# A two-block network on one core: gated-recurrence levels raised in two pairs of buffers and multiplied two by two; top-k masks formed by ScalarE

## The reference

```python
def dsa_mixer(...):                       # selected attention, 4 heads of 64
    s = einsum(q_idx, k_idx); score = sum_h w * relu(s)      # 8 index heads of 32
    score = where(causal, score, -1e30)
    _, sel = top_k(score, 128)            # only these keys are attended to
    logits = q.k * 64**-0.5, -1e30 where not valid; softmax; times v

def hgrn2_mixer(...):                     # recurrent heads, 4 of 128, chunks of 64
    G = cumsum(log_f) within a chunk
    A[i,j] = sum_d q[i,d] exp(G[i,d]-G[j,d]) k[j,d]   for j <= i
    o = A v + (q exp(G)) S ;  S = exp(G_last) S + (k exp(G_last-G))^T v
    rmsnorm(o) * silu(g)
```

## Time and profile before

| | |
|---|---|
| time, median of 3 runs | 1200.15 us (1198.34 to 1200.52) |
| the profiled execution | 1199.26 us, span 1197.5 us |
| busy share of the span | PE 99%, PEld 81%, DVE 67%, ACT 57%, POOL 38% |
| index scores and top-k to the start of the recurrent products | about 575 to 680 us |
| recurrent windows 0, 1, 2, 3 | about 680 to 705, to 739, to 777, to 805 us |
| mean granted TensorE clock | 0.998 |

### The profile page before, as it was taken

One profiled execution on the slowest core, in us unless ns is written; L12 is line 12 of the kernel. 1 busy time (PEld: TensorE's weight loads), 2 busy tenths in 40 slices (PEclk: granted clock), 3 DMA queues, 4 the chain that ended last, 5 costly groups with the idle time before them and its releaser, 6 DMA issues.

```text
span 1197.5 us, 19754 instructions
## 1 busy us (share of the span) xinstructions
PE 1183.4 (99%) x7102; PEld 964.1 (81%) x7102; DVE 807.4 (67%) x1839; ACT 687.8 (57%) x1333; POOL 459.0 (38%) x300
## 2 busy tenths in 40 slices
PE   9999999999999999999999999999999999999998
PEld 8777777777877777789777677778988889899897
DVE  6866767776777776766689866776761265475575
ACT  6766666675546778734567787653532353443542
POOL 0201111112520000053477697315354577576663
PEclk9999999999999999999999999999999999999999
DMA  5423354541543322352322112323363323223322
GB/s 202 159 71 106 91 174 141 159 159 53 194 121 113 95 96 92 121 160 71 114 71 71 37 54 71 123 89 120 128 193 106 106 71 118 94 100 112 106 72 71
DMA packets 41040, 131.82 MB, mean 110 GB/s; under 512 B 4576, under 2 KB 7264, under 8 KB 40944
## 3 DMA queue, kind: packets, MB, share of 16 engines
q1 hardware_dynamic: 35360, 121.39, 31.6%
q10 hardware_dynamic: 5584, 9.18, 2.5%
HBM read 127.10 MB, written 2.13 MB: 108 GB/s over the span
## 4 chain that ended last, share of the span: by engine, by line
PE 84%; DVE 8%; issue 4%; DMA 2%; ACT 2%; POOL 1%; SPq 0%; ACTq 0%; DVEq 0%; POOLq 0%
PE G L1069 17%; PE G L1071 16%; PE G L1070 16%; DVE adaw L3144 2%; PE G L2118 2%; PE S L1196 2%; PE G L2119 2%; PE G L2120 2%; DVE best L3143 2%; PE O L1256 2%; PE T L1235 2%; PE S L1413 1%; PE O L1476 1%; PE T L1460 1%; PE S L2119 1%
## 5 line engine op out<-in xcount | busy, mean ns | idle before, releaser
L1069 PE MATMUL G<-hi,wH 128*128 128x512 f32 x1032 | 419.0, 406 | 0.5 <-DVE xT L1164 0.4
L1071 PE MATMUL G<-hi,wL 128*128 128x512 f32 x1032 | 403.3, 391 | 0.0
L1070 PE MATMUL G<-lo,wH 128*128 128x512 f32 x1032 | 403.0, 390 | 0.0
L633 POOL TENSOR_TENSOR wL<-w,wH 128x1024 fp32r<-128x1024 f32 x89 | 219.9, 2476 | 440.1 <-ACT wH L2273 440.0
L1069 PEld LDWEIGHTS G<-hi,wH 128*128 128x128 f32 x1032 | 194.0, 188 | 55.6 <-issue 17.5
L1071 PEld LDWEIGHTS G<-hi,wL 128*128 128x128 f32 x1032 | 193.9, 188 | 42.2
L1070 PEld LDWEIGHTS G<-lo,wH 128*128 128x128 f32 x1032 | 194.4, 188 | 38.3 <-issue 1.9
L2273 ACT ACTIVATE wH<-w 128x1024 fp32r<-128x1024 f32 x140 | 147.2, 1054 | 103.8 <-DMA w<-weights_dram 53.8
L413 POOL TENSOR_TENSOR kd<-kd,band 128x256 f32<-128x256 f32 x8 | 6.5, 808 | 195.4 <-DMA kd<-c_dram 195.4
L2832 DVE TENSOR_TENSOR wL<-w,wH 128x1024 fp32r<-128x1024 f32 x51 | 62.3, 1222 | 11.0 <-ACT wH L2273 10.2
L1186 DVE CUSTOM_DVE_ANT_0 adaw<-adaw,scr 128x1024 f32<-128x1024 f32 x36 | 62.2, 1727 | 0.0
(11 more groups left out here) (560 smaller groups left out, 2564.8 us busy)
## 6 DMA issues: line engine op xcount, KB each, us to landing
w<-weights_dram SPq DMA_DIRECT2D x150, 512.0 KB, 3.6
adaw<-ada_dram SPq DMA_DIRECT2D x48, 512.0 KB, 4.3
wp<-weights_dram SPq DMA_DIRECT2D x20, 512.0 KB, 4.4
kd<-c_dram ACTq DMA_DIRECT2D x16, 512.0 KB, 4.8
xT<-x_dram SPq DMA_DIRECT2D x4, 512.0 KB, 8.1
out_dram<-xT SPq DMA_DIRECT2D x8, 256.0 KB, 2.2
scr<-ca_dram SPq DMA_DIRECT2D x2, 512.0 KB, 6.3
kd<-cbias SPq DMA_DIRECT2D x8, 128.0 KB, 4.4
```

What stands on the lines that cost most here:

```text
L633: g.tensor_tensor(wL[:, u.slot], raw_home(u), wH[:, u.slot].bitcast(f32), ALU.subtract).then_inc(w_lo, 1)
L1069: mm(home[:, :], whi, H[:, k, :], start=(k == first), stop=False)
L1070: mm(home[:, :], whi, L[:, k, :], start=False, stop=False)
L1071: last = mm(home[:, :], wlo, H[:, k, :], start=False, stop=(k == final))
```

## The change

- `raised(t, n)` names one of two pairs of rows: the first pair for n = 1, 2, 3, 6, 7, the second for n = 4, 5, 8. The raises n = 3, 5, 7 read one pair and write the other, so they don't wait for the product of their level; the half that they don't touch is copied by ACT (`leave`, three for each head, 128x512).
- PE makes the products 3 and 4 back to back, 5 and 6 too, and `turn_ke` directly behind product 7. The pieces of units between them are joined.
- DVE's and ACT's orders in the windows are rewritten: among others `silu_z(t)` and `gates(t + 1)` come after the joins of levels 5 and 6, and `rooted_h` before raise 4.
- The masks of selected attention: DVE's TENSOR_SCALAR is removed, ACT computes -x - 3e38 in place (`masks_c`), and `logits_c` waits for it. `scores_c(0)` moves two k-tiles into unit 11; `exps_c(2)` and `exps_c(3)` move ahead of other ACT work; two convolution taps move behind the last softmax turn.

```diff
+        def raised(t, n):
+            row = 2 - 2 * (t % 2) + (4 if n in (4, 5, 8) else 0)
+            return kd[:, row, :], kd[:, row + 1, :]
...
         def logits_c(dve, k):
             t, r = C_TURNS[k]
+            dve.wait_ge(*mark("i_mask", 3 - r))
...
+        def masks_c(act, q):
+            act.wait_ge(*mark("i_best", q))
+            part = sel[:, A_AT[q]:A_AT[q] + (q + 1) * P]
+            s.activation(part, part, ACT.Identity, scale=-1.0, bias=lowest[:, 0:1]).then_inc(sem("i_mask"), 1)
...
             def product(t, p):
                 pe.wait_ge(sem("h_x"), 8 * t + max(p, 1) + since("h_x"))
+                if p in (4, 6):
+                    pe.wait_ge(*mark("h_moved", 3 * t + p // 2 - 1))
...
             def first_window():
-                gemm_h(1, 0, (5,))
+                gemm_h(1, 0, (5, 6, 7))
                 product(0, 3)
-                gemm_h(1, 0, (6, 7))
                 product(0, 4)
-                gemm_h(1, 1, (0, 1))
+                gemm_h(1, 1, (0, 1, 2, 3))
                 product(0, 5)
-                gemm_h(1, 1, (2, 3))
                 product(0, 6)
-                gemm_h(1, 1, (4, 5))
+                gemm_h(1, 1, (4, 5, 6))
                 product(0, 7)
-                gemm_h(1, 1, (6, 7))
+                turn_ke(0)
+                gemm_h(1, 1, (7,))
...
             def window(t):
                 opened(t)
                 fill(t, 3)
+                fill(t, 4, (0, 1))
                 product(t, 3)
+                product(t, 4)
                 if t == 2:
                     conv_sum()
-                fill(t, 4)
-                product(t, 4)
+                fill(t, 4, (2, 3))
                 fill(t, 5)
                 product(t, 5)
+                product(t, 6)
                 if t == 2:
                     conv_sqsum()
                 fill(t, 6)
-                product(t, 6)
                 fill(t, 7, (0, 1))
                 product(t, 7)
+                turn_ke(t)
                 fill(t, 7, (2, 3))
...
             gemm_i(10)
+            gemm_i(11, (0, 1))
             scores_c(pe, 0)
-            gemm_i(11)
+            gemm_i(11, (2, 3, 4, 5, 6, 7))
...
+            def leave(t, n):
+                m = 1 << (n - 1)
+                act.wait_ge(sem("h_x"), 8 * t + n + since("h_x"))
+                if n == 3 and t > 1:
+                    act.wait_ge(sem("h_o"), t - 1 + since("h_o"))
+                s.activation(left_behind(t, m, n + 1), left_behind(t, m, n), ACT.Copy).then_inc(sem("h_moved"), 1)
...
                 terms(CONV_C[5], CONV_C[6])
+                leave(0, 3)
                 take_hv(0)
                 gate_1(0)
+                leave(0, 5)
                 conv_terms(0, 0)
                 split_h(4)
+                leave(0, 7)
                 forget(1)
...
                 conv_terms(t, 4)
+                leave(t, 5)
                 raw_h(t, 3, zraw, sem("h_silu"), t + since("h_silu"))
                 gate_1(t)
...
             def raise_both(t, n):
                 m = 1 << (n - 1)
-                dve.wait_ge(sem("h_products"), 8 * t + (2 if n == 1 else n + 1) + since("h_products"))
+                if n in (1, 2, 4, 6):
+                    dve.wait_ge(sem("h_products"), 8 * t + (2 if n == 1 else n + 1) + since("h_products"))
+                if n in (4, 6):
+                    dve.wait_ge(*mark("h_moved", 3 * t + n // 2 - 1))
...
-                link(v.tensor_scalar(part, part, -HUGE, NEG, ALU.not_equal, ALU.mult))
...
-                level_of(t, 2)
...
+                raise_both(t, 2)
+                raise_both(t, 3)
+                joined(t, 2)
...
+                else:
+                    rooted_h(t - 1)
+                raise_both(t, 4)
+                joined(t, 3)
+                if t == 2:
+                    conv_centre()
+                raise_both(t, 5)
+                joined(t, 4)
...
+                normed_h(t - 1)
+                raise_both(t, 6)
+                raise_both(t, 7)
+                joined(t, 5)
+                joined(t, 6)
                 gated_h(t - 1)
                 if t < 3:
                     silu_z(t)
+                    gates(t + 1)
```

More of the change, by code:

```diff
@@ L226, in build @@
         epsc = sb("epsc", [P, 1])
+        lowest = sb("lowest", [P, 1])
         vecT = sb("vecT", [P, N_VEC])
@@ L1897, in turn_ke @@
                 pe.wait_ge(sem("h_x"), 8 * t + 8 + since("h_x"))
+                pe.wait_ge(*mark("h_moved", 3 * t + 3))
                 pe.wait_ge(sem("h_v"), t + 1 + since("h_v"))
                 for c in range(3):
-                    last = nc.tensor.transpose(T[0][:, c * P:(c + 1) * P], raised(t)[1][:, c * P:(c + 1) * P], ident[:, :])
+                    last = nc.tensor.transpose(T[0][:, c * P:(c + 1) * P], raised(t, 8)[1][:, c * P:(c + 1) * P], ident[:, :])
                 last.then_inc(sem("h_keT"), 1)
@@ L1930, in outputs @@
                 for c in range(1, NQ):
-                    mm(O[:, c * P:(c + 1) * P], state[:, c - 1, :], raised(t)[0][:, c * P:(c + 1) * P], start=False, stop=False)
+                    mm(O[:, c * P:(c + 1) * P], state[:, c - 1, :], raised(t, 8)[0][:, c * P:(c + 1) * P], start=False, stop=False)
                 pe.wait_ge(sem("h_early"), t + 1 + since("h_early"))
@@ L2037, in last_window @@
                 opened(3)
-                fill(3, 3, (0, 1))
+                fill(3, 3)
                 product(3, 3)
-                fill(3, 3, (2, 3))
                 product(3, 4)
                 output_m(0, (4, 5))
+                output_m(1, (4, 5))
                 product(3, 5)
-                output_m(1, (4, 5))
                 product(3, 6)
                 output_m(0, (0, 1))
+                output_m(1, (0, 1))
                 product(3, 7)
-                output_m(1, (0, 1))
                 turn_ke(3)
@@ L2518, in _ @@
             raw(8)
+            masks_c(act, 1)
             terms(CONV_I[1], CONV_I[2])
@@ L2528, in attend_c @@
             def attend_c():
+                masks_c(act, 2)
                 exps_c(act, 1)
@@ L2547, in attend_c @@
                 split_h(3)
-                terms(CONV_C[3], CONV_C[4])
+                masks_c(act, 3)
+                terms(CONV_C[3], CONV_C[3] + 1)
                 exps_c(act, 4)
@@ L2553, in attend_c @@
                 take_turned_c(act, 5)
+                terms(CONV_C[3] + 1, CONV_C[4])
                 widen_c(act, 0)
@@ L2583, in keys @@
                     act.wait_ge(sem("h_keT"), t - 1)
-                s.activation(raised(t)[1], klog, ACT.Exp, scale=-1.0).then_inc(sem("h_k"), 1)
+                s.activation(raised(t, 1)[1], klog, ACT.Exp, scale=-1.0).then_inc(sem("h_k"), 1)
             def queries(t):
@@ L2667, in window @@
                         silu_scalar_2(act, "cv", k, cv_th[k])
+                leave(t, 3)
+                if t == 3:
                     for k in range(2):
@@ L2682, in window @@
                         s.activation(csq[:, k, :], cacc[:, k, :], ACT.Square).then_inc(sem("conv_sq"), 1)
-                gated_h(t - 1)
                 if t < 3:
                     forget(t + 1)
+                leave(t, 7)
                 split_h(4 * t + 4)
+                gated_h(t - 1)
                 if t < 3:
@@ L3143, in _ @@
                     link(v.max(best[:, n % 2, :], part))
-                    link(v.match_replace(part, best[:, n % 2, :], part, -HUGE))
+                    if n < TOPK // 8 - 1:
+                        link(v.match_replace(part, best[:, n % 2, :], part, -HUGE))
+                    else:
+                        v.match_replace(part, best[:, n % 2, :], part, -HUGE).then_inc(sem("i_best"), 1)
                     between(q, n)
-                link(v.tensor_scalar(part, part, -HUGE, NEG, ALU.not_equal, ALU.mult))
             def clamped(t):
@@ L3251, in first_window @@
                 joined(0, 1)
-                level_of(0, 2)
+                raise_both(0, 2)
+                raise_both(0, 3)
+                joined(0, 2)
                 low_c(dve, 0)
-                level_of(0, 3)
+                raise_both(0, 4)
+                joined(0, 3)
+                raise_both(0, 5)
+                joined(0, 4)
                 low_c(dve, 1)
-                for n in range(4, 7):
-                    level_of(0, n)
+                raise_both(0, 6)
                 raise_both(0, 7)
+                joined(0, 5)
+                joined(0, 6)
                 gates(1)
```

41 lines of the change are left out of this document (15 added, 26 removed).

## The result

The changed kernel takes 1204.54 us (median of 7 runs, 1202.84 to 1207.22), the kernel before took 1198.88 us beside it (7 runs, 1196.73 to 1200.52). The ratio is 1.0053, 95% interval 1.0039 to 1.0067: slower by 5.7 us in the medians, where 1203.0, 2.9 us above the kernel before, was forecast. The profiled execution took 1204.54 us with a span of 1202.7 us and a mean granted clock of 0.995 (before: 1199.26, 1197.5, 0.998).

What follows compares the result with a forecast made beforehand. PE's own order of work was taken to set the time (84% of the chain). -3.0 - 3.6 + 3.4 + 5.6 - 2.4 + 2.0 + 0.9 = +2.9 us on the median 1200.15, stated as 1203.0; range 1197.8 to 1206.8.

Steps and rivals of the forecast that it cites:

- Term 1: Selected attention: masks on ACT and moved scores and exps remove PE's waits; 3.0 us won, bounds 1.5 to 3.8.
- Term 2: Four windows: joining products two by two saves PE's restarts, 0.9 us per window, 3.6 us won.
- Term 3: Window 0: ACT gets late with its copies, so PE waits at updates(0); +3.4 us, bounds 1.0 to 4.5.
- Term 4: Windows 1 and 2: PE's unit waits for silu_z behind product 6, 3.5 and 2.1 us; +5.6, bounds 4.5 to 6.5.
- Term 5: States of window 2: PE, now later, no longer waits and the clock drop behind goes; -2.4 us, bounds -2.6 to 0.
- Term 6: Clock drops behind the three new waits, 1.5 us each, none to three of them; +2.0 us, bounds 0 to 4.5.
- Term 7: Window 3: delays for the z copy (0.5) and turned keys (0.4) cancel the joins' 0.9; +0.9 us, bounds 0 to 1.5.
- faster rival: Windows 1 and 2: the z step doesn't hold PE, so its wait and clock drops go; 1196.1 us, chance 0.13.

Runs made afterwards that it cites:

- orders mended: The three waits mended run, plus ACT's window-0 key steps ahead of three taps, DVE's states_of ahead of queries_1, raw_h and gate_1 ahead of level 5's copy: 1191.77 us.
- three waits mended: Changed kernel with silu_z ahead of raise 6, forget(1) ahead of level 7's copy, convolution scaling behind the states, take_ke right behind take_first: 1196.46 us.
- recurrent heads alone: Changed kernel without the selected-attention part, masks on DVE as before: 1207.91 us, ratio 1.0076 to the kernel before.
- five waits mended, products apart: The orders mended run with PE's order of the kernel before: a piece of a unit between any two products, turn_ke in the next window; 1201.79 us.
- masks alone, second run: Kernel before with only the selected-attention part (masks on ACT and its small shifts), measured once more: 1196.31 us, ratio 0.9963.

## Why the prediction was right

The mechanism, the places and the direction were right, the size was not: 2.9 us was forecast and the medians differ by 5.7. That 1203.0 lies only 1.5 below the 1204.54 measured is in part luck, as the kernel before took 1198.88 us beside the changed one, 1.3 less than the 1200.15 from which the forecast was counted. In the profiled executions the spans differ by 5.2 us, 2.3 over the forecast: the clock drop was priced 0.75 too low, the other terms of the four windows come to 0.9 together, and 0.6 lies outside the change. Measured by window, the stretch of the change is 4.56 us longer (131.90 - 124.39 = 7.51 in the windows, less 2.95 ahead of them), against a sum of 2.9; the rest of the profile's difference of 5.2 us lies outside it: a clock drop at 324 to 332 us in the execution that was profiled, +1.24 by 616 us, and -0.6 behind 810.

- *Term 1, the masks, -3.0.* Product 0 starts at 678.29 against 680.00, in a trace that is 1.24 us later before the change begins: 2.95 won. By themselves the masks gave 3.8 us. The total is right, but not its items. The 0.5 that was counted as part of the wait for the logits isn't: that group takes 1.64 us without the wait too. And a wait of 0.51 for `queries_2` is new. What makes up for most of these is something that the prediction had only in its upper bound: the transposes at 649.12 and at 657.94, which took 1.36 us (with a wait of 0.33) and 1.04 to the next group, take 0.74 and 0.75 now. That gains and losses nearly cancel is luck.
- *Term 2, the joins, -3.6.* Products 0.52 us apart; four windows with the orders mended are 4.5 us shorter than before, of which 0.9 is the wait for the states and about 1.5 the drop behind it, less the 1.4 us of waits that are left; 3.5 remain for the joins. The pair of runs with the products together and apart gives 4.0.
- *Term 3, window 0, +3.4, with its joins +2.5.* Measured +2.95, from waits of 2.97 and 0.63. Its cause holds: filling ACT's wait for the raise took 0.8 us off PE's waits here, copying the keys ahead of `keys`, `factor` and the exps a further 1.6 (with 1.09 for the states new in its place), and taking the last taps out of the way the rest.
- *Term 4, the z step, 3.5 and 2.1.* Measured 3.70 and 1.77. Putting it ahead of raise 6 left 0.59 and nothing, so the chain behind product 6 is the cause. The sentence that no order of other engines can shorten it stands for other engines; the order of DVE itself could.
- *Term 5, what is given back, -2.4.* Neither PE's wait for the states nor the clock drop of the earlier trace rows is there. This held by 0.12 us, and only because PE was late by itself: DVE has the states done at 781.79, and PE's matmuls that read them start at 781.91. As soon as the z waits went, the same chain on DVE held PE for 3.9 us; two of its scaling steps met a split of POOL there (2.89 and 2.54 us), in the changed kernel one (2.56).
- *Term 6, the clock, +2.0.* One drop, within the bounds, but its price was 1.5 in the prediction and is 2.75 here: the 18 matmuls from 727.14 to the product at 734.19 took 7.05 us, where they take 4.30 at full clock (722.86 to 727.16 in the run with three waits mended). The sentence of the Trainium skill that term 6 names says which level is the default; that waits as short as these lead back to it was the prediction's own step, and this trace agrees with that step once in three.
- *Term 7, window 3, +0.9.* Window 3 is 0.94 us shorter: the joins' 0.9 and the 1.5 of the old clock drop, less the wait of 0.92 for z and 0.5 more. The sum of the terms there was -1.5. Of the two delays that term 7 added, that for z was 0.92 and not 0.5, and PE had no wait for the turned keys.

Held against the forecast by window: +0.45 in window 0, +1.0 in window 1, -0.4 in window 2, +0.56 in window 3, and nearly nothing in the masks. Of window 1's excess 0.75 is the clock.

The faster rival (the z step doesn't hold PE) could not have come true by the z step alone: with its waits gone the time stayed at 1205.23 us. That rival was priced at 1196.1 by taking a wait off PE's line without asking which chain is late next, and the expectation of that run made the same mistake.

## What to carry to other kernels

Before two steps of the critical engine are merged, lay out what the other engines do between them: the time that was there for a raise, a copy or a z step is work that hid them, and the merge pays only if their orders are refitted with it (here -4.5 us against +9). When a wait is removed, compute the next late chain before the gain is written down; on this kernel three of them stood one behind the other. By the medians, taking the first away (the z step) gave nothing by itself, the second (the scaling ahead of the states) 5.7 us, the third (the copy of the turned keys) 3.0, and the waits left after it 4.7. If a change made of parts is slower, run the parts: one of these two was worth keeping as it was.

## What the runs showed of the hardware

**The clock behind a wait doesn't follow from the wait's length alone.** The same wait of about 3 us (2.82 to 3.00) in window 0 was followed by full clock in the profile of the changed kernel (1.00 from 700 to 705) and by the lower level for part of the next 5 us in five other kernels (granted 0.61 from 700 to 704 with the z step early, and 0.66 from 700 to 705 here, with the recurrent heads alone):

```profile
700.00:705.00 5.00, 4.32 (x15) 3.78 (x16) 4.34 (x13) 4.94 (x9) 2.82 (x3) 0.66 0.00 2
```

A wait of 1.77 us was followed by none, one of 1.41 us (five waits mended, products apart, 706.24) by a drop, and one of 0.95 us (masks alone, second run, 773.54) too:

```profile
774.00:776.00 2.00, 2.00 (x21) 1.76 (x21) 1.38 (x3) 1.94 (x4) 0.00 (x0) 0.81 0.06 25
776.00:778.00 2.00, 2.00 (x31) 1.86 (x28) 0.41 (x1) 1.78 (x4) 0.00 (x0) 0.50 0.00 0
```

What decides between them stays open. The price can be read twice: window 0 is 28.42 us with the wait and no drop, 29.99 with the same wait and a drop (1.6 us), and the drop in window 1 cost 2.75. The masks alone were profiled twice, and both profiles show the drop (the other behind a wait of 0.96 us, granted 0.62 and 0.52 from 778 to 782); every other kernel has one profile, so whether a given wait of it is followed by a drop in every execution isn't shown.

**Some DVE steps that read SBUF end with POOL's weight split, others beside it don't.** The rows of the masks and of the convolution's scaling show it for TENSOR_SCALAR and for SCALAR_TENSOR_TENSOR with both large inputs in SBUF: 0.49 becomes 2.54 us, 0.75 becomes 2.89. MAX8 and MATCH_REPLACE8, which read SBUF too, take their usual 0.69 and 0.68 us within a split of POOL (kernel before):

```profile
648.27 2.38 POOL L633 TENSOR_TENSOR wL<-w,wH 128x1024 fp32r<-128x1024 f32 x1 [2.28 <-ACT wH L2273]
```

```profile
648.81 0.68 DVE L3144 MATCH_REPLACE8 adaw<-best,adaw 128x512 f32<-128x512 f32 x1
649.52 0.69 DVE L3143 MAX8 best<-adaw 128x8 f32<-128x512 f32 x1
```

The Trainium skill (SBUF — State Buffer, "SBUF: two separate sides") says that some DVE operations and a GpSimd operation take a pair of ports that they share by an exclusive lock, for the whole instruction. The trace agrees, by the ends of the slowed steps, 0.3 to 0.6 us behind those of the splits; and the z step, which reads PSUM in windows 1 and 2, took 0.67 to 0.69 us there in every run, also within a split (changed kernel, 767.20, against POOL's 766.72 to 769.10).
